# Moving rows of the gathered tiles between three stages of an expert layer: five dots and six early rows fewer ahead, six late rows more behind

## The reference, cut to what matters

```python
def chunk(ht):                      # 128 tokens
    q = (ht @ w_q).reshape(PEER_CHUNK, PEER_HEADS, 2, PEER_HALF)
    s = jnp.einsum('thpc,hpnc->thpn', q, subkeys)
    sv, si = lax.top_k(s, PEER_TOPK)                  # 16 keys of each half
    ... # the 16 best pairs of 8 heads: 128 experts for each token
    gate = jax.nn.softmax(top_s, axis=-1)
    act = jax.nn.gelu(jnp.einsum('thkd,td->thk', u[expert], ht), approximate=False)
    return jnp.einsum('thk,thkd->td', (gate * act), v[expert])
```

## Time and profile before

| what | value |
|---|---|
| median of 3 runs | 2577.65 us (2576.46 to 2580.89) |
| the profiled execution | 2577.02 us, its span 2575.0 us |
| mean granted TensorE clock | 0.993 |
| busy: TensorE, VectorE, GpSimd, ScalarE | 98%, 82%, 59%, 34% |
| moved | 763.35 MB, mean 296 GB/s |

### The profile page before, as it was taken

One profiled execution on the slowest core, in us unless ns is written; L12 is line 12 of the kernel. 1 busy time (PEld: TensorE's weight loads), 2 busy tenths in 40 slices (PEclk: granted clock), 3 DMA queues, 4 the chain that ended last, 5 costly groups with the idle time before them and its releaser, 6 DMA issues.

```text
span 2575.0 us, 41533 instructions
## 1 busy us (share of the span) xinstructions
PE 2513.7 (98%) x15177; PEld 2247.5 (87%) x15177; DVE 2116.4 (82%) x4504; ACT 879.8 (34%) x1658; POOL 1509.7 (59%) x1046
## 2 busy tenths in 40 slices
PE   8999989999999999998999999998999999999998
PEld 6777768999999999998999999987888888888887
DVE  7022273699999999999999997789998999989998
ACT  4223252322222222234777773232222222222222
POOL 2111030346777778886666668856665676666663
PEclk9999999999999999998999999999999999999999
DMA  4110022337899999998999999999999999999995
GB/s 155 49 33 25 26 89 99 123 111 233 308 337 335 351 330 357 347 341 304 395 398 394 400 401 410 400 380 377 381 375 380 367 379 379 376 379 369 377 374 212
DMA packets 296672, 763.35 MB, mean 296 GB/s; under 512 B 25824, under 2 KB 116320, under 8 KB 293728
## 3 DMA queue, kind: packets, MB, share of 16 engines
q0 software_dynamic: 110592, 402.70, 41.7%
q1 hardware_dynamic: 161280, 288.81, 31.9%
q10 hardware_dynamic: 24672, 70.33, 7.1%
HBM read 669.47 MB, written 92.27 MB: 296 GB/s over the span
## 4 chain that ended last, share of the span: by engine, by line
PE 66%; DVE 12%; POOL 4%; DMA 3%; issue 1%; ACT 1%; SPq 0%; another core or an unknown queue 0%; DVEq 0%; ACTq 0%
PE bank L1793 25%; PE bank L2199 19%; PE wide L2199 13%; DVE u_row L1469 5%; PE bank L2167 3%; PE bank L2020 3%; PE bank L2077 2%; POOL w_lo L718 2%; POOL u_row L735 2%; DMA g_first<-g_d 1%; DVE rest_k L1436 1%; DVE ix L1439 1%; POOL u_row L730 1%; DVE ix L1442 1%; DMA u_row<-in_u_rows,ids 1%
## 5 line engine op out<-in xcount | busy, mean ns | idle before, releaser
L786 POOL DMA_INDIRECT d_row<-in_v,ids x330 | 564.2, 1710 | 297.0 <-DVE yg L1691 225.2
L1793 PE MATMUL bank<-h_hi,w_hi 128*128 128x320 f32 (+1 forms) x2368 | 557.1, 316 | 8.6 <-POOL w_lo L718 7.9
L1793 PE MATMUL bank<-h_hi,w_lo 128*128 128x320 f32 (+1 forms) x2368 | 546.5, 312 | 0.0
L1793 PE MATMUL bank<-h_lo,w_hi 128*128 128x320 f32 (+1 forms) x2368 | 546.3, 312 | 0.1
L718 POOL TENSOR_TENSOR w_lo<-w_raw,w_hi 128x512 fp32r<-128x512 f32 (+1 forms) x230 | 367.1, 1614 | 178.3 <-DVE gate_j L1611 95.4
L730 POOL DMA_INDIRECT u_row<-in_u_rows,ids x384 | 403.7, 1051 | 110.9 <-issue 82.2
L1469 DVE CUSTOM_DVE_ANT_0 u_row<-wide,u_row 128x1024 f32<-128x1024 f32 x384 | 449.6, 1220 | 10.3 <-DMA u_row<-in_u_rows,ids 6.2
L1691 DVE SCALAR_TENSOR_TENSOR yg<-d_row,uh,yg 128x1024 f32<-128x1024 f32 x330 | 409.8, 1277 | 1.5
L1793 PEld LDWEIGHTS bank<-h_hi,w_hi 128*128 128x128 f32 x2368 | 395.4, 189 | 14.4 <-POOL w_lo L718 7.5
L1793 PEld LDWEIGHTS bank<-h_lo,w_hi 128*128 128x128 f32 x2368 | 399.2, 189 | 2.9 <-issue 0.4
L1793 PEld LDWEIGHTS bank<-h_hi,w_lo 128*128 128x128 f32 x2368 | 398.7, 189 | 2.5
(11 more groups left out here) (234 smaller groups left out, 4131.1 us busy)
## 6 DMA issues: line engine op xcount, KB each, us to landing
w_raw<-in_u SPq DMA_DIRECT2D x128, 512.0 KB
v_raw<-in_v ACTq DMA_DIRECT2D x126, 512.0 KB
act_d<-act_st SPq DMA_DIRECT2D x128, 320.0 KB
g_d<-g_st SPq DMA_DIRECT2D x20, 2048.0 KB
a_raw<-act_d SPq DMA_DIRECT2D x154, 256.0 KB
g_raw<-g_d SPq DMA_DIRECT2D x120, 256.0 KB
w_raw<-in_w_q SPq DMA_DIRECT2D x32, 512.0 KB
w_raw<-in_w_in SPq DMA_DIRECT2D x20, 512.0 KB
```

The source lines that it names most:

```text
L786: nc.gpsimd.indirect_dma_start(d_row[k % DR][:, :], None, v_rows, bass.IndirectOffsetOnAxis(ids[:, c:c + 1], 0)).then_inc(d_in[k % DR], 16)
L1793: ins = pe.matmul(banks[h][:, 0:n], lhs[:, part], rhs[:, k, h * n:(h + 1) * n], start=(k == 0 and lhs is lhs_hi and rhs is h_hi), stop=(k ...
```

## The change

```diff
-TILE_DOTS = (3, 3, 3, 3, 3, 3, 3, 4)
+TILE_DOTS = (3, 3, 3, 3, 3, 3, 3, 3)
...
-EARLY = 27
+EARLY = 24
...
+ROWS_UNIT_MORE = (2, 2, 2, 2, 2, 3, 2, 3, 2, 2)
+MORE_GROUPS = 6
...
-    by_group = [ROWS_UNIT0, *[ROWS_UNIT] * (NG - 2), ROWS_UNIT_LAST]
+    by_group = [ROWS_UNIT0, *[ROWS_UNIT] * (NG - 2 - MORE_GROUPS), *[ROWS_UNIT_MORE] * MORE_GROUPS, ROWS_UNIT_LAST]
```

## The result

The changed kernel took 2588.3 us (median of 8 runs, 2585.1 to 2593.8) against 2579.1 for the kernel before on the same chip (8 runs, 2570.1 to 2585.2). The ratio is 1.0039, 95% interval 1.0024 to 1.0055: slower by 9 us, where 5.3 us of gain were forecast. It lies outside the range, on the other side. The profiled execution took 2588.4 us, span 2586.5; that of before 2577.0 and 2575.0, so the two traces differ by 11.5 us, some 2 more than the medians do.

A forecast was written before the change was run, and what follows sets the result against it. TensorE was taken as the bound, rarely waiting from 600 us on, with VectorE full beside it in dense routing and strips. −1.1 − 2.3 − 1.9 = −5.3 from 2577.0 gave 2571.7, as median 2572.3 us; range 2568.8 to 2577.3.

The forecast's parts named there:

- the four dots ahead of the gates: Dense tiles' routing: four dots fewer on VectorE bring the gates earlier; −2.3 us, bounds 0 and −4.6.
- the first rival: Ahead of the gates: rows come too late and VectorE stays bound to their landings; −1.1 to −2.5, 2575.7 us; chance 0.24.
- no net change, but a scatter of as much in the supply: Dense tiles' routing: earlier `eq` products meet other GpSimd gathers on the shared port, each costing GpSimd the same 1.9 us.
- transport: Late groups: 375 GB/s is all the DMAs yield, six rows cost 8.4 us, 2580.8; chance 0.06 alone, 0.05 with late rows.
- Items themselves come earlier: Dense tiles' routing: a gather fewer behind item 45 and GpSimd's 1.74 us ring wait gone, so later asks come earlier.
- of the 7.9 us I expect 1 to 3 back: TensorE's waits for lowered weights, 7.9 us from 600 us on, were to shrink by 1 to 3 us.
- The dot behind the gates: Hand-over: three dots instead of four behind the gates, so the first table is copied earlier; −1.1 us.
- the clock: Hand-over: TensorE keeps full clock, so VectorE's 1.85 us wait for the third turn goes; −1.85 us, bounds 0 and 1.85.
- Nothing hides it: Hand-over: TensorE stands waiting for the first table, so the dot's 1.14 us counts in full.
- The strips and the rest of the first product: Stages behind the hand-over: same dots and gathers in the strips, idle VectorE time after them; 0, transport bound −1.3 us.
- Six late rows: Late groups: six more rows of 1.28 us on VectorE, 7.7 us without cover, covered by its idle time; 0.
- The late gather: Gather k = 2 waits for the third last item, so row DMAs start some 4 us earlier; 0, bounds ±1.3 us.

The follow-up runs named there:

- e2: The change with 25 dots per dense tile as before, so only the rows move (48 early, 336 late): 2577.7 us, ratio 0.9997 to the kernel before.
- e4: The kernel before with asks for rows in the dense tiles' routing one higher (+ 6 for + 5): 2583.9 us, ratio 0.9999.
- e11: The kernel before with asks for rows in the dense tiles' routing one lower (+ 4 for + 5): 2586.2 us, ratio 1.0020.
- e3: The change with asks for rows in the dense tiles' routing one lower (+ 4 for + 5): 2575.9 us, ratio 0.9979 to the kernel before.
- e1: The kernel before with only the dense tiles' dots changed, last place three for four (24 dots), rows as before: 2593.7 us, ratio 1.0051.
- e6: The change with GpSimd lowering only 64 of each 512 columns in the dense tiles' routing: 2564.5 us, ratio 0.9943 to the kernel before.
- e7: The kernel before with GpSimd lowering only 64 of each 512 columns in the dense tiles' routing: 2568.7 us, ratio 0.9960.
- e9: The change with an item's lowering in the dense tiles' routing as four subtractions of 256 columns for two of 512: 2581.8 us, ratio 1.0004.
- e5: The change with a dense tile's missing dot taken from the fourth place instead of the last: 2579.2 us, ratio 1.0002 to the kernel before.
- e12: The change with a dense tile's missing dot taken from the first place instead of the last: 2580.9 us, ratio 1.0000 to the kernel before.
- e8: The change with asks for rows in the dense tiles' routing two lower (+ 3 for + 5): 2578.1 us, ratio 0.9988 to the kernel before.

## Why the prediction was wrong

**The step that failed** is the term for the four dots ahead of the gates (−2.3, bounds 0 and −4.6), which took every other instruction of VectorE as long as before. What stands on this in the prediction is one sentence behind the first rival, on the shared port: "no net change, but a scatter of as much in the supply". I priced the lock on one side, GpSimd's gathers, and took the number of meetings as given. The same lock holds VectorE, which was full in that stage, and what meets what changed when the dots moved. Instead of 0 to 4.6 us less, the stage took 13.4 us more: VectorE's five groups cost 21.3 us more, against which the whole change had 7.6 to win. The rows to see it by were in the trace of before: `eq` at a mean of 3473 ns, while the same instruction on the same shape took 2.3 us when alone. A group whose mean lies half above its shortest was a price already being paid, 16 us of it, and a change that shifts that group in time sets it anew. None of my rivals had this, and the one that ended slower (transport) was another mechanism.

**The four dots ahead of the gates**. Not gained: the gates' division began at 1181.16 for 1164.73, 13.4 us of it from the stage and 3.1 from its later beginning. The reason was not late rows, for the dots waited 1.5 us in the whole stage. "Items themselves come earlier" was wrong, and with it "of the 7.9 us I expect 1 to 3 back": it became 19.6, ring waits 39.7 for 8.5.

**The dot behind the gates** (−1.1) and **the clock** (−1.85) came out near their numbers in these two traces, but the reason given is only a part of it. VectorE after:

```profile
1181.16 4.25 DVE L1575 TENSOR_TENSOR route<-route,gsum 128x1024 f32<-128x1024 f32 x1
...
1188.77 0.35 DVE L1580 COPY gate_g<-route 128x384 f32<-128x384 f32 x1
1189.15 0.89 DVE L1584 COPY route_t<-bank 128x384 f32<-128x384 f32 x2
...
1193.04 0.88 DVE L1584 COPY route_t<-bank 128x384 f32<-128x384 f32 x2
```

TensorE:

```profile
1185.47 0.77 PE L2145 MATMUL bank<-ident,route 128*128 128x128 f32 x5 [0.83 <-DVE route L1575]
...
1189.76 0.77 PE L2145 MATMUL bank<-ident,route 128*128 128x128 f32 x5 [1.78 <-DVE route_t L1584]
```

From the division's start to the first copy of a table it is 7.99 us for 10.14: the dot's 1.14, and 1.1 from the copy of the gates, 0.35 us for 1.44 (unforeseen). TensorE stands 0.83 + 1.78 for 4.01 us, the clock is 1.00 in this stretch where it was 0.50, and the third copy (1193.04) waits for nothing where 1.85 us stood ahead of it. But the hand-over of before was itself stretched by the lock. GpSimd beside it, before:

```profile
1165.25 2.55 POOL L718 TENSOR_TENSOR w_lo<-w_raw,w_hi 128x512 fp32r<-128x512 f32 x2
...
1172.28 2.34 POOL L718 TENSOR_TENSOR w_lo<-w_raw,w_hi 128x1024 fp32r<-128x1024 f32 x1
```

The division (4.17 us from 1164.73) ends 1.1 us behind the first of these, the copy of the gates (1.44 from 1173.39) 0.2 us behind the second. Where nothing holds them they take 1.22 and 0.35 us; the copy, though it has a single input, is held all the same. e2 has the four dots of before and meets neither:

```profile
1167.52 1.23 DVE L1575 TENSOR_TENSOR route<-route,gsum 128x1024 f32<-128x1024 f32 x1
...
1173.23 0.45 DVE L1580 COPY gate_g<-route 128x384 f32<-128x384 f32 x1
1173.72 0.89 DVE L1584 COPY route_t<-bank 128x384 f32<-128x384 f32 x2
```

There the first copy comes 6.20 us behind the division's start, TensorE waits at none of its three turns, and the clock is 1.00 from 1167 to 1185. e4, with four dots too, is the same; e11, whose division (3.01 us) and copy (1.58) are held again, has the wait of 4.01 us again. So the wait that I read as four dots' work was of the same kind as the loss, and "Nothing hides it" holds for the dot only where that wait stands. From the division's start to the end of the span it is 1405.3 us for 1410.3, but the 14 traces give 1402.3 (e3) to 1412.9 (e1, with the dots of the change) for it; what of these 4.9 us belongs to the terms can't be told.

**The strips and the rest of the first product** (0): TensorE 99.98 of 100 and 127.37 of 128 us. Right.

**Six late rows** (0) and **transport**: TensorE has 300.00 of 300 us, VectorE 273.73 for 267.81, 5.9 us more for 5.5 rows of 1.28 (7.0), and 382 GB/s are moved for 375. Right, and e2 (0.9997) says the same; the rival in which transport ends at 375 falls. **The late gather** gave no effect that can be told.

Without the lowering in the way the change is worth about what the sum says: e6 against e7 gives −4.2. That the numbers lie so near is luck in part, since in their traces the stage gave 3.8 and the hand-over had no wait to give. As a forecast the sum was not good, since the term left out had four times its size.

**What stays open.** That the lock turns meetings into lost time is shown by e6, e7 and e9. That ring releases keep the engines in step is argued from the timelines and from e5 and e12, and not shown; the ring waits and the five groups rise together over most of the table (e8 and e9 less so, and not where the lowering is cut), but no experiment set the phase alone. What a given table of dots will draw can't be told from this: the change is worth +9 us with asks of + 5, −10 with + 4 (e3 against e11, 2575.9 − 2586.2), and −4 where the lowering is cut. What of the 10 us of scatter between executions is of the same kind was not tried.

## What to carry to other kernels

Before pricing a schedule edit on a full engine, compare each group's mean with its shortest instance: where it lies well above, look for another engine that shuts the group out. Where there is one, moving work by a microsecond can cost or win several times what was moved. Price such an exclusion on both engines, above all on the one that is full, and also where a wait that you want to shorten is made. Count all instructions that can meet the other engine: in e5 one group got shorter and its neighbour longer. If two engines exclude each other, short instructions on the one that has room spare the other, at a price of their own; and a gain measured under one placing of the work isn't the gain under the next.

## What the hardware showed unexpectedly

- An instruction of 0.27 us was held for 2.34, nearly both subtractions of 1.26 us that stood back to back on GpSimd. None of the eight `eq` that met the lowering in the change got in between the two. With four of 0.72 they mostly did (`eq` 2.69 us in the mean for 3.92), but one `low_b` of 0.29 us there took 2.85, through all four.
- The `eq` of 1040.64 has a recorded start 0.26 us ahead of the lowering at 1040.90, and yet lasted 4.93 us, about the 2.3 of its own and the lowering's 2.52. Two more in the change are like it (976.54 and 991.97). In all three a gather of GpSimd was running at the recorded start, and the lowering followed it at once. In e5 the `eq` of 1023.44 starts 0.17 us ahead of a lowering with GpSimd idle, and takes 2.29 us, and the lowering 3.27 for 1.3. So the recorded start alone doesn't tell who gets the port; that the gather decides it wasn't tested.
- GpSimd's indirect gathers pay too. All those of over 2 us in this stage (9 before, 10 after, most of them 2.83 us for 0.94) begin while an `eq` runs and end 0.82 to 0.83 us behind it. Their mean is 1085 ns before and 1093 after, 994 with the lowering cut, and 993 in e5, where the lowering is whole but the `eq` end early.
